# Compressed attention branch: plain fp32 value and denominator products replaced by five products of rounded parts

## The reference, cut to what matters

```python
k_cmp = rope(compress(kc.reshape(kvshape), pe_k, w1_k, w2_k), cmp_end)
v_cmp = compress(vc.reshape(kvshape), pe_v, w1_v, w2_v)
...
s_c = jnp.einsum('bqghd,bngd->bghqn', qb, k_cmp)
p_c = masked_softmax(s_c, cmp_end[None, :] <= t[:, None])
o_c = jnp.einsum('bghqn,bngd->bqghd', p_c.astype(v_cmp.dtype), v_cmp)
...
o = gb[..., 0:1] * o_c + gb[..., 1:2] * o_s + gb[..., 2:3] * o_w
```

## Time and profile before

| what | value |
|---|---|
| median of 3 runs | 3108.62 us (3103.97, 3108.62, 3113.73) |
| profiled execution | 3110.92 us, of which the span from first to last instruction is 3108.8 us |
| mean granted TensorE clock | 0.971 of 2.4 GHz |
| PE busy | 2927.6 us, 94% |
| DVE busy | 2014.5 us, 65% |
| ACT busy | 1513.5 us, 49% |
| attention of layer 0 | from about 262 to 785 us |

### The profile page before, as it was taken

One profiled execution on the slowest core, in us unless ns is written; L12 is line 12 of the kernel. 1 busy time (PEld: TensorE's weight loads), 2 busy tenths in 40 slices (PEclk: granted clock), 3 DMA queues, 4 the chain that ended last, 5 costly groups with the idle time before them and its releaser, 6 DMA issues. The chain is left out here.

```text
span 3108.8 us, 35729 instructions
## 1 busy us (share of the span) xinstructions
PE 2927.6 (94%) x12484; PEld 2206.0 (71%) x12484; DVE 2014.5 (65%) x3618; ACT 1513.5 (49%) x2626; POOL 327.8 (11%) x255
## 2 busy tenths in 40 slices
PE   7999999999999999999998775789999999999999
PEld 5885666556777888878876564455587788887887
DVE  6656555554477776677666699744347867667665
ACT  5454555555354444445433667444535444444444
POOL 2560000000300000000012134320030000000000
PEclk9999999999999999999999888899999999999999
DMA  5253122211433333323323023541142333332332
GB/s 174 67 144 82 46 53 49 56 49 32 143 91 97 95 91 101 95 89 101 96 68 118 1 65 116 161 114 42 31 146 88 95 96 94 102 95 89 105 102 85
DMA packets 357770, 277.15 MB, mean 89 GB/s; under 512 B 58213, under 2 KB 308135, under 8 KB 357079
## 3 DMA queue, kind: packets, MB, share of 16 engines
q1 hardware_dynamic: 356439, 272.78, 29.8%
q10 hardware_dynamic: 1152, 2.10, 0.2%
HBM read 238.18 MB, written 34.02 MB: 88 GB/s over the span
## 5 line engine op out<-in xcount | busy, mean ns | idle before, releaser
L504 PE MATMUL PS<-HH,WH 128*128 128x512 f32 (+1 forms) x2160 | 851.7, 394 | 56.5 <-POOL WL L477 29.5
L505 PE MATMUL PS<-HL,WH 128*128 128x512 f32 (+1 forms) x2160 | 844.2, 391 | 0.0
L506 PE MATMUL PS<-HH,WL 128*128 128x512 f32 (+1 forms) x2160 | 843.6, 391 | 0.0
L504 PEld LDWEIGHTS PS<-HH,WH 128*128 128x128 f32 x2160 | 410.2, 190 | 152.7 <-issue 47.2
L506 PEld LDWEIGHTS PS<-HH,WL 128*128 128x128 f32 x2160 | 409.9, 190 | 85.5
L505 PEld LDWEIGHTS PS<-HL,WH 128*128 128x128 f32 x2160 | 410.5, 190 | 83.3 <-issue 1.4
L493 DVE TENSOR_TENSOR WL<-WR,WH 128x1024 fp32r<-128x1024 f32 x280 | 341.8, 1221 | 49.2 <-ACT WH L486 44.7
L486 ACT ACTIVATE WH<-WR 128x1024 fp32r<-128x1024 f32 x280 | 297.6, 1063 | 117.9 <-PE PS L506 90.0
L960 ACT ACTIVATE n_PX<-PS 128x512 f32<-128x512 f32 (+1 forms) x320 | 172.9, 544 | 217.8 <-PE PS L921 110.7
L1064 DVE CUSTOM_DVE_ANT_0 n_JUNK<-PS,n_MZ 128x512 bf16<-128x512 f32 (+2 forms) x320 | 147.1, 488 | 93.9 <-PE PS L852 93.8
L473 POOL TENSOR_TENSOR TOUCH<-WR 128x1 f32<-128x1 f32 x55 | 20.2, 367 | 1745.0 <-DVE WL L493 786.7
(11 more groups left out here) (386 smaller groups left out, 5125.9 us busy)
## 6 DMA issues: line engine op xcount, KB each, us to landing
WR<-in_ffn_w_up SPq DMA_DIRECT2D x176, 512.0 KB, 3.8
WR<-in_ffn_w_down SPq DMA_DIRECT2D x88, 512.0 KB, 3.4
WH<-qh_save SPq DMA_DIRECT2D x64, 256.0 KB
n_RB<-r_save SPq DMA_DIRECT2D x96, 128.0 KB, 3.1
WL<-ql_save SPq DMA_DIRECT2D x32, 256.0 KB
WR<-in_nsa_w_out SPq DMA_DIRECT2D x16, 512.0 KB, 5.3
WR<-in_dsa_w_in SPq DMA_DIRECT2D x16, 512.0 KB, 4.2
WR<-in_dsa_w_out SPq DMA_DIRECT2D x16, 512.0 KB, 4.5
```

Of the source, the lines that this page charges most:

```text
L504: nc.tensor.matmul(dst, wh, xh, start=start, stop=False)
L505: nc.tensor.matmul(dst, wh, xl, start=False, stop=False)
L506: return nc.tensor.matmul(dst, wl, xh, start=False, stop=stop)
```

## The change

The cmp unit's plain products are replaced. VectorE makes two F32R tiles from the probabilities PX: `PH`, their rounded value, and `PL`, what is left. `VCH` and `VCL` are the same parts of the compressed values; `ONB` becomes F32R (ones need no low part). TensorE then makes three products for the values and two for the denominators. In the preparation VectorE builds `VCL` (one clearing and four subtractions) at the seventh query block. The tile that was called GL (low part of the hidden layer of the compression) is dropped, and `VCL` serves for it first.

```diff
             if n.kind == "cmp":
-                probs = B["PX"][:, u % 4, :]
+                c = a.plan.compressed.index(u)
+                high, low = B["PH"][:, :], B["PL"][:, :]
+                pe.wait_ge(sem0["part_high"], 2 + c + 1)
                 pe.wait_ge(a_ov, a.ov0 + n.g - 1)
-                nc.tensor.matmul(bank(6), B["VC"][:, g, :], probs, start=True, stop=True)
+                nc.tensor.matmul(bank(6), B["VCH"][:, g, :], high, start=True, stop=False)
+                nc.tensor.matmul(bank(6), B["VCL"][:, g, :], high, start=False, stop=False)
+                pe.wait_ge(sem0["part_low"], 2 + c + 1)
+                nc.tensor.matmul(bank(6), B["VCH"][:, g, :], low, start=False, stop=True)
                 pe.wait_ge(a_ov, a.ov0 + n.g)
-                last = nc.tensor.matmul(bank(7), B["ONB"][:, :], probs, start=True, stop=True)
+                nc.tensor.matmul(bank(7), B["ONB"][:, :], high, start=True, stop=False)
+                last = nc.tensor.matmul(bank(7), B["ONB"][:, :], low, start=False, stop=True)
...
+        def probability_parts_dve(dve, a, u):
+            c = a.plan.compressed.index(u)
+            probs, high, low = a.B["PX"][:, u % 4, :], a.B["PH"][:, :], a.B["PL"][:, :]
+            dve.wait_ge(a_ex, a.qk0 + u + 1)
+            if c:
+                dve.wait_ge(a_pv, a.qk0 + a.plan.compressed[c - 1] + 1)
+            nc.vector.tensor_scalar(high, probs, 1.0, 0.0, ALU.mult,
+                                    ALU.add).then_inc(sem0["part_high"], 1)
+            dve.wait_ge(sem0["part_high"], 2 + c + 1)
+            nc.vector.tensor_tensor(low, probs, high.bitcast(F32),
+                                    ALU.subtract).then_inc(sem0["part_low"], 1)
...
                 if a.n == 1 and s in LATE_MASKS:
                     mask_dve(dve, *LATE_MASKS[s])
+                if s in plan.compressed:
+                    probability_parts_dve(dve, a, s)
                 for rb in plan.sums_at.get(s, ()):
...
+                if k == 7:
+                    dve.wait_ge(S["c2"], 2)
+                    link(nc.vector.memset(N["VCL"][:, :, :].bitcast(F32), 0.0))
+                    dve.wait_ge(a_ready, 1)
+                    for g in range(2):
+                        src = PS[64 * g:64 * g + 64, 5, 0:DH]
+                        for h in range(2):
+                            dst = (slice(64 * h, 64 * h + 64), g, slice(DH * h, DH * h + DH))
+                            link(nc.vector.tensor_tensor(N["VCL"][dst], src, N["VCH"][dst].bitcast(F32),
+                                                         ALU.subtract))
```

More of the change, by code:

```diff
@@ L159, in __init__ @@
         self.closes = {u.rb: x for x, u in enumerate(self.units) if u.last}
+        self.compressed = [x for x, u in enumerate(self.units) if u.kind == "cmp"]
         self.place_peaks()
@@ L274, in trunk @@
                 ("KCA", [P, 2, 3 * DH], F32R), ("KCB", [P, 2, 3 * DH], F32R),
-                ("VS", [P, 2, QT, P], F32), ("VW", [P, 2, QT, P], F32), ("VC", [P, 2, P], F32),
-                ("ONB", [P, P], F32), ("G4", [P, 2, 3 * NH, 4], F32)):
+                ("VS", [P, 2, QT, P], F32), ("VW", [P, 2, QT, P], F32), ("VCH", [P, 2, P], F32R),
+                ("VCL", [P, 2, P], F32R), ("ONB", [P, P], F32R), ("G4", [P, 2, 3 * NH, 4], F32)):
             N[name] = sb("n_" + name, shape, dt, scope)
@@ L290, in trunk @@
                 ("XH", [P, 2, 4, 2, DH], F32R), ("XL", [P, 2, 4, 2, DH], F32R),
-                ("GH", [P, 2, P], F32R), ("GL", [P, 2, P], F32R),
+                ("GH", [P, 2, P], F32R),
                 ("W2F", [P, 2, 2, DH], F32), ("W2H", [P, 2, 2, 2, DH], F32R),
@@ L313, in trunk @@
         attention_buffers(N, "n_", 3, 3)
+        N["PH"] = sb("n_PH", [P, HALF], F32R, inner)
+        N["PL"] = sb("n_PL", [P, HALF], F32R, inner)
         inner.close()
@@ L1693, in trunk @@
             "trig", "consts", "zero", "ev", "rope", "rh", "rl", "vtr", "vdone", "gs", "gex", "xf", "xh", "xl",
-            "gelu", "gh", "gl", "c2", "c2ev", "w2", "w2h", "w2l", "chain")}
+            "gelu", "part_high", "part_low", "c2", "c2ev", "w2", "w2h", "w2l", "chain")}
         KEY_TILES = {2: ("KSA", "KSB"), 4: ("KWA", "KWB")}
@@ L1830, in compress @@
                 pe.wait_ge(S["w2l"], 1)
-                pe.wait_ge(S["gl"], kv + 1)
-                GH, GL = N["GH"], N["GL"]
+                pe.wait_ge(S["part_low"], kv + 1)
+                GH, GL = N["GH"], N["VCL"]
                 for ht in range(2):
@@ L1943, in gelu @@
                 act.wait_ge(S["gelu"], kv + 1)
[L1944 removed]
+                nc.scalar.activation(N["GH"][:, :, :], GF, ACT.Copy).then_inc(S["part_high"], 1)
             def rotated(k):
@@ L1985, in prep0_act @@
                         src = PS[64 * g:64 * g + 64, 5, 0:DH]
-                        nc.scalar.activation(N["VC"][0:64, g, 0:DH], src, ACT.Copy)
-                        last = nc.scalar.activation(N["VC"][64:128, g, DH:2 * DH], src, ACT.Copy)
+                        nc.scalar.activation(N["VCH"][0:64, g, 0:DH], src, ACT.Copy)
+                        last = nc.scalar.activation(N["VCH"][64:128, g, DH:2 * DH], src, ACT.Copy)
                     last.then_inc(a_ready, 1)
@@ L1996, in prep0_dve @@
             nc.vector.memset(N["MZ"][:, P:4 * P], 0.0)
-            nc.vector.memset(N["ONB"][:, :], 0.0)
-            nc.vector.memset(N["VC"][:, :, :], 0.0)
+            nc.vector.memset(N["ONB"][:, :].bitcast(F32), 0.0)
+            nc.vector.memset(N["VCH"][:, :, :].bitcast(F32), 0.0)
             nc.vector.memset(N["KCA"][:, :, :].bitcast(F32), 0.0)
@@ L2068, in gelu_low @@
             def gelu_low(kv):
-                dve.wait_ge(S["gh"], kv + 1)
-                nc.vector.tensor_tensor(N["GL"][:, :, :], GF, N["GH"][:, :, :].bitcast(F32),
-                                        ALU.subtract).then_inc(S["gl"], 1)
+                dve.wait_ge(S["part_high"], kv + 1)
+                nc.vector.tensor_tensor(N["VCL"][:, :, :], GF, N["GH"][:, :, :].bitcast(F32),
+                                        ALU.subtract).then_inc(S["part_low"], 1)
             def turned(k):
```

6 lines of the change are left out of this document (3 added, 3 removed).

## The result

The changed kernel takes 3127.01 us (median of 6 runs, 3120.67 to 3132.73), the kernel before in the same job 3107.6 us: ratio 1.0065, 95% interval 1.0051 to 1.0079. Run again in two other jobs it had 1.0054 (1.0041 to 1.0067) and 1.0043 (1.0028 to 1.0058). It is slower by some 15 to 20 us, where 3.4 were forecast.

A forecast was written before the change was run, and what follows sets the result against it. It took TensorE's time plus its short waits as the bound. Seven losses of 1.0 us less nine gains of 0.40 us gave +3.4 us, 3112.0 us against the median 3108.62, range 3104 to 3120.

The forecast's parts named there:

- The loss in a step with peaks: Seven cmp steps: TensorE waits for VectorE's parts behind the fourth peak; 1.0 us more each, 7.0 us in all.
- a gain of 0.38 in the denominators: Nine cmp steps without peaks: denominators go from 0.955 to 0.56 us, 0.40 us less each, 3.6 us in all.
- the preparation: VectorE's added clearing and four subtractions, at most 2.2 us, hidden where VectorE waits 2.96 us for ScalarE; cost zero.
- The sum of +3.4: Whole kernel: seven losses of 1.0 us less nine gains of 0.40 us make +3.4 us.
- The rival in which the loss does not come: Steps with peaks: VectorE's parts come in time, each step gains 0.60; 7.8 us less in all, 3100.8 us; chance 8%.
- the granted clock is 1.00: Layer 0's attention: clock read at its 2.4 GHz level over the 523 us window of the kernel before.
- in steps without peaks VectorE is free: Nine cmp steps: VectorE makes both parts before TensorE's value products need them, so they are hidden.
- the steps without peaks lose as well: Rival: VectorE delayed beyond its cover through DMA and ScalarE, TensorE waits; about +17 us, 3126 us; chance 7%.
- 1.35 us of cover: Steps without peaks: values start this long before the denominators, leaving VectorE room to come 1.3 to 2.1 us later.
- it is passed on: Steps without peaks: the 0.40 us gain carries on, as ScalarE's bank 6 copy and next value product follow the denominators.
- nothing later gives the loss back: Steps with peaks: the 1.0 us loss stays, because the next TensorE wait hangs on the same delayed product.
- The range: Whole kernel's time: 3104 to 3120 us, with 0.85 chance of lying within 0.3% of before.

The follow-up runs named there:

- e11: Changed kernel with five unneeded F32R products in the high-part wait of steps with peaks and GpSimd's splits released later; ratio 1.0041 to before.
- e4: Changed kernel with VectorE's parts ahead of the step's peaks and GpSimd's splits released later; 3105.24 us beside 3107.43, ratio 1.0000.
- e9: The changed kernel unaltered, run again in another job; 3126.5 us, ratio 1.0054 to the kernel before.
- e2: Changed kernel with five unneeded F32R products filling TensorE's wait for the high part in steps with peaks; ratio 1.0047 to before.
- e14: e12 once more: kernel before, plain products kept, with VectorE's unused parts and TensorE's waits for them; ratio 1.0053.
- e7: e4 without the clearing and four subtractions that make the low part of the compressed values; ratio 0.9999 to before.
- e12: Kernel before, plain products kept, with VectorE's parts computed but unused and TensorE waiting for them; ratio 1.0044.
- e1: Changed kernel with VectorE making the two parts ahead of the step's peaks instead of behind them; ratio 1.0012 to before.
- e3: Changed kernel with GpSimd's splits waiting for the cmp values of rounds 14 and 15 instead of the scores; 3126.85 us, ratio 1.0063.

## Why the prediction was wrong

**Right.** The loss in a step with peaks (0.99, forecast 1.0); the high part, 0.42 (forecast 0.43, though its shape stood in no row); the low part, 0.69; the wait, 1.11 (forecast 1.0 to 1.3); no wait for VectorE in the steps without peaks of rounds 0 to 12, and a gain of 0.38 in the denominators (forecast 0.40); the products 0.235 apart where nothing holds them, not the 131 ns of the Trainium skill ("TensorE: Matmul & The Clock Gate", Back-to-back issue gap); the preparation, in the trace 1.3 us of VectorE's time in a gap (0.27 of clearing, 0.99 of subtractions; at 206.25, one query block later than the prediction placed it) and nothing in the runs. The sum of +3.4 is found in e11 as +4.0 net of the peak waits. The rival in which the loss does not come was worked out at -7.8; e4, which is that case, has -6.8 net.

**The step that failed: the clock.** The prediction read "the granted clock is 1.00" off the kernel before, took the time to be "TensorE's time plus the short stretches in which it waits", and so priced each new wait at its own length, with 2.4 GHz behind it. The runs show 1.2 GHz behind 14 of the 21 new waits of 1.1 us in the changed kernel's three profiles. The largest missing term is 5 x 1.36 = 6.8 us (4 x 1.36 in e9). It is in no rival. e2 takes it away without shortening a step, e14 brings it back with the old products. The Trainium skill ("TensorE: Matmul & The Clock Gate", A second HAM failure mode: psum-queue depth-cycling) tells of a kernel whose TensorE idles shortly between groups of products, and whose clock swings between the levels. The prediction cited that page for another figure and passed this over; the traces agree with it, with falls in 5, 4 and 5 of seven steps.

**A second miss: GpSimd.** The prediction said that in steps without peaks VectorE is free. It looked at round 2 and, for the latest arrival, at round 12, but not at rounds 14 and 15, where GpSimd's splits begin. The last two rounds cost 5.6 us of distance (3.5 in e9), the falls of the clock behind the wait included. The rival "the steps without peaks lose as well" had the place but not the mechanism: it looked for lateness through DMA and ScalarE. Each of these steps has the 1.35 us of cover that was worked out; the low part is 2.0 us longer there.

**A third: "it is passed on" and "nothing later gives the loss back".** The gain of the steps without peaks is partly taken back some 14 us later. VectorE waits there for a DMA, and the peaks stand behind it. The same place in the kernel before, and in e7, whose TensorE gains in every step:

```profile
414.02 0.59 ACT L983 ACTIVATE n_DR<-PS 1x512 f32<-1x512 f32 x1
...
427.33 0.69 DVE L1099 TENSOR_TENSOR n_TMP<-n_OP,n_RB 128x512 f32<-128x512 f32 x1 [2.09 <-DMA n_RB<-r_save]
...
429.15 0.33 PE L852 MATMUL PS<-n_KWA,WH 128*128 128x128 f32 x1 [1.44 <-DVE n_NM L1064]
```

```profile
416.13 0.59 ACT L997 ACTIVATE n_DR<-PS 1x512 f32<-1x512 f32 x1
...
429.51 0.69 DVE L1125 TENSOR_TENSOR n_TMP<-n_OP,n_RB 128x512 f32<-128x512 f32 x1 [2.46 <-DMA n_RB<-r_save]
...
431.32 0.33 PE L860 MATMUL PS<-n_KWA,WH 128*128 128x128 f32 x1 [1.81 <-DVE n_NM L1078]
```

The DMA's chain begins with ScalarE's copy of the near sums, ahead of the cmp denominators, at 414.02 and 416.13 (the first rows); from there to VectorE's operation it is 13.31 and 13.38 us. TensorE, 0.38 quicker behind that copy, waits 0.37 longer. In the table: 10.4 to 11.2 us of peak waits in e4 and e7 against 7.0 in the mean of before, and so e4 gains 6.8 net and 2.6 in distance. Not all of this is the DMA's: 1.3 us come from the fourth peaks, which wait 0.64 instead of 0.45 behind the early parts, seven times; 2.5 are left in the mean of e4 and e7. For the changed kernel it is 8.4 against 7.0, 1.4 us. These waits also hold the scatter of the kernel before: its four distances span 5.2 us, and without them 0.9. That the DMA sets them is read from the traces; no run moved it. The waits outside the cmp steps are 4.7 to 6.0 us in the changed kernel's three profiles and 1.9 to 6.8 in the four of before, so single profiles overlap; e12 and e14, whose denominators are not quicker, have 2.3 and 3.0, which fits.

**The base.** The profile that the sum was made against has the longest distance of the four; against the mean, 496.8, the changed kernel's three (513.05) are 16.3 longer. Of the total, 3.4 was forecast, 6.4 is the clock (mean of 5, 4 and 5 steps), 4.8 the last two rounds with GpSimd, 1.4 the peak waits, together 16.0. The medians of the runs say 14.6 to 19.4. Only e1 (1.0012) and e4 (1.0000) show a cause in the time itself, and there the loss, the clock and, in e4, GpSimd go away together; how the 16 us divide among them is read from the traces. **The range** was made of costs of instructions alone, with no term for what an idle engine does to its own clock.

## What to carry over

A wait of one microsecond put in front of a dense TensorE can cost more than itself: here 1.0 us of lost time brought 1.4 more in two of three cases, so in a place like this price it at up to twice its length, or put the producer's instructions ahead of the work that delays them (e1), which here took away all but 0.1% of a loss of 0.4 to 0.65%. When a helper engine gets new work in a repeated step, look at every repetition, the last ones too, for another engine that starts there. And a gain ahead of a fixed chain (here a DMA of some 13 us) is worth only as much as the wait behind that chain leaves.

## What the runs showed of the hardware

- The granted clock fell to 1.2 GHz after TensorE had waited once for 1.11 us in an else dense stretch, in 24 of 35 such steps of the changed order, in 5 of 14 with plain products, and in 0 of 14 with products in the wait. It did not fall at the peak waits of 1.44 in the kernel before and 1.81 in e7, so the length of one wait does not decide it.
- VectorE beside GpSimd: 0.42 became 0.96, 0.69 became 2.73; with GpSimd moved away (e3) they took 0.43 and 0.69.
- A VectorE operation with one input and a rounded output takes 0.42 us for 128x512, as fast as the slope of plain fp32 outputs gives.
